# Who rounds the weight slabs while the gates are built: GpSimd alone, or ScalarE the high halves and GpSimd the low ones

## What is computed

```
experts, gates = top 16 of the key products, for 8 heads      # 128 picks for each token
a   = einsum('cd,ced->ce', h_c, u[e_c])                       # one dot product for each pick
act = gelu(a) * g_c
out = einsum('ce,ced->cd', act, v[e_c])
```

## Time and profile before

| | |
|---|---|
| time of 3 runs | 2722.94 to 2726.37 us, median 2724.3 |
| the profiled execution | 2727.47 us, its span 2725.7 us |
| granted TensorE clock, mean | 0.97 |
| PE busy | 2557.2 us (94%) |
| DVE busy | 1528.9 us (56%) |
| ACT busy | 725.1 us (27%) |
| POOL busy | 1786.2 us (66%) |
| DMA | 502.61 MB, mean 184 GB/s |

### The profile page before, as it was taken

How to read it: one execution, slowest core, us unless ns; L and a number is a source line. 1 busy time by engine, 2 the same in 40 slices (tenths; PEclk the granted TensorE clock), 3 DMA queues, 4 the chain that set the end, 5 groups by cost and what they waited for, 6 DMA issues and landing times.

```text
span 2725.7 us, 35334 instructions
## 1 busy us (share of the span) xinstructions
PE 2557.2 (94%) x12644; PEld 2132.2 (78%) x12644; DVE 1528.9 (56%) x3197; ACT 725.1 (27%) x1297; POOL 1786.2 (66%) x1315
## 2 busy tenths in 40 slices
PE   3989799999989999998889998999999989999999
PEld 2866568888757666677768898999999978888887
DVE  5447632121246325445438898877778366666665
ACT  5148511000132323433310111111212123333332
POOL 2746557666824243366556676999998668888885
PEclk8989899999989999999999998999999999999999
DMA  6224222222311011122223345899987799999995
GB/s 245 93 70 148 101 77 93 93 103 98 108 48 62 31 47 66 47 92 79 78 81 118 119 146 197 291 366 357 345 337 296 273 365 346 342 341 352 352 353 219
DMA packets 134761, 502.61 MB, mean 184 GB/s; under 512 B 11248, under 2 KB 53872, under 8 KB 103152
## 3 DMA queue, kind: packets, MB, share of 16 engines
q1 hardware_dynamic: 70832, 311.97, 31.4%
q0 software_dynamic: 36864, 134.23, 13.0%
q10 hardware_dynamic: 26944, 54.85, 5.3%
HBM read 448.58 MB, written 52.43 MB: 184 GB/s over the span
## 4 chain that ended last, share of the span: by engine, by line
PE 61%; DVE 11%; POOL 10%; DMA 9%; issue 5%; ACT 3%; ACTq 0%; SPq 0%; DVEq 0%; POOLq 0%
PE banks L566 9%; PE banks L567 9%; PE banks L568 9%; DMA raw<-weights 4%; POOL W_lo L503 3%; POOL W_lo L426 3%; PE banks L694 3%; DMA B_lo_plain<-u_rows,arena 3%; PE banks L924 2%; PE banks L926 2%; PE banks L925 2%; PE banks L839 2%; PE banks L841 2%; PE banks L840 2%; PE banks L712 2%
## 5 line engine op out<-in xcount | busy, mean ns | idle before, releaser
L451 POOL TENSOR_TENSOR W_lo<-raw,W_hi 128x512 fp32r<-128x512 f32 x376 | 493.9, 1323 | 0.0
L454 POOL TENSOR_TENSOR beat<-zero 128x1 f32<-128x1 f32 x94 | 19.8, 211 | 615.8 <-PE banks L714 215.5
L839 PE MATMUL banks<-A_hi,W_hi 128*128 128x384 f32 x1024 | 381.0, 372 | 1.2 <-issue 1.1
L841 PE MATMUL banks<-A_hi,W_lo 128*128 128x384 f32 x1024 | 346.4, 338 | 0.0
L840 PE MATMUL banks<-A_lo,W_hi 128*128 128x384 f32 x1024 | 344.5, 336 | 0.0
L426 POOL TENSOR_TENSOR W_lo<-raw,W_hi 128x2048 fp32r<-128x2048 f32 x65 | 299.4, 4606 | 5.2
L566 PE MATMUL banks<-A_hi,W_hi 128*128 128x512 f32 x680 | 267.8, 394 | 4.9 <-issue 4.9
L568 PE MATMUL banks<-A_hi,W_lo 128*128 128x512 f32 x680 | 264.7, 389 | 0.0
L567 PE MATMUL banks<-A_lo,W_hi 128*128 128x512 f32 x680 | 264.6, 389 | 0.0
L446 POOL CAST W_hi<-raw 128x512 fp32r<-128x512 f32 x376 | 247.9, 674 | 0.0
L1877 DVE TENSOR_TENSOR A_lo<-arena,A_hi 128x768 fp32r<-128x768 f32 x64 | 136.6, 2134 | 171.5 <-ACT A_hi L1362 171.4
(11 more groups left out here) (282 smaller groups left out, 6185.0 us busy)
## 6 DMA issues: line engine op xcount, KB each, us to landing
raw<-weights SPq DMA_DIRECT2D x241, 1024.0 KB, 4.9
gelu_dram<-B_plain ACTq DMA_DIRECT2D x64, 384.0 KB
gates_dram<-arena ACTq DMA_DIRECT2D x48, 512.0 KB, 10.0
arena<-gelu_dram SPq DMA_DIRECT2D x32, 768.0 KB, 8.4
arena<-gates_dram SPq DMA_DIRECT2D x32, 768.0 KB, 11.1
W_plain<-weights SPq DMA_DIRECT2D x4, 1024.0 KB, 15.9
X<-x_t SPq DMA_DIRECT2D x1, 2048.0 KB, 14.4
arena<-v_rows,arena POOLq DMA_INDIRECT x128, 7.9
```

What stands on the lines that cost most here:

```text
L451: return pool.tensor_tensor(W_lo[:, j, cols], raw[:, j, cols], W_hi[:, j, cols].bitcast(F32), ALU.subtract)
L839: mm(to, lh, rh, start=k == 0, stop=False)
L841: last = mm(to, ll, rh, start=False, stop=k == KD - 1)
```

## The change

From slab 111 on (`HIGHS_AT`), the high half of a u slab, and of the first two v slabs, is made by ScalarE with an activation (`high_of`), which signals a new semaphore `u_high`. GpSimd waits for it and makes the low half. ScalarE makes the high half of slab s+1 before the gelus of slab s. That is behind the gelus of slab s-1 and behind the two gate stores that follow them in half of the slabs; for slabs 155 and 156 it is also behind a set of four stores. Slabs up to 110 stay as they were.

```diff
+HIGHS_AT = HOT_AT + 1
...
-        slab_half, v_half = sem("slab_half"), sem("v_half")
+        slab_half, u_high, v_half = sem("slab_half"), sem("u_high"), sem("v_half")
...
             for s in range(IN_PARTS, N_MID + PAIRS + 2):
-                split_whole(s)
+                if s < HIGHS_AT:
+                    split_whole(s)
+                else:
+                    pool.wait_ge(u_high, s - HIGHS_AT + 1)
+                    low_of(s)
                 if s >= HOT_AT and n_u < SLOTS:
...
+            def high_of(s):
+
+                j = s % 2
+                act.wait_ge(slab_loaded[j], (s - j) * 8 + (8 * (N_ADA - 4) + 16))
+                act.wait_ge(slab_used, s - 1)
+                act.activation(W_hi[:, j, :], raw[:, j, :], ACT.Copy).then_inc(u_high, 1)
+
...
                 for s in range(with_tokens):
+                    high_of(N_MID + first + s + 1)
                     gelus(first + s, tokens=lambda j: tokens(2 * s + j))
                     if q:
                         per_slab = STORES // 4
...
                 for s in range(between):
                     for part in range(STORES // 2 * s, STORES // 2 * (s + 1) if s < 2 else 0):
                         store_gates(q, part)
+                    high_of(N_MID + first + with_tokens + s + 1)
                     gelus(first + with_tokens + s)
                 first += with_tokens + between
+            high_of(N_MID + PAIRS + 1)
             act.wait_ge(u_dotted, SLOTS)
             act.activation(dots, dots, ACT.Gelu).then_inc(dots_gelu, 1)
```

## The result

The changed kernel takes 2737.97 us (median of 5 runs, 2736.42 to 2742.55) against 2725.14 us for the kernel before (5 runs, 2722.94 to 2726.93): ratio 1.0052, 95% interval 1.0041 to 1.0062. By the medians it is slower by 12.8 us (11 to 17 by the interval). The forecast was 2729.7 with a range up to 2737.0. The sign held, and so did the mechanism in the gates' stage, with a loss larger than forecast. In the tail, behind the gates' stage, the forecast had nearly all of the delay absorbed, and it was not.

The account below looks back on a forecast made before the run. It took TensorE, at 10.25 us a slab, to bound the gates' stage, with 6.7 us lost to late one-hots. Profiled 2727.47 + 4.4 (stage) + 1.0 (third v slab) = 2732.9; the median lies 3.2 lower: 2729.7, range 2719 to 2737.

Parts of the forecast that it names:

- The quantity that counts is the distance from a slab's end to the first fetch: Gates' stage: late fetched rows delay dots and one-hots, so this distance sets TensorE's stalls; B + 6.8 to B + 9.2 before.
- B: The end of slab s-2, which frees the place of slab s; the prediction counts the stage's times from it.
- First fetch at B + 7.8, store slabs B + 9.1: Gates' stage after the change: GpSimd's first fetch behind cast and low half, later in slabs with gate stores.
- A fetch of 8.6 in store slabs: Gates' stage: assumed length of a first fetch in store slabs, the middle of 7.9 to 9.3 us; 6.25 in others.
- it evens out: Rival, no change: traffic sets fetch landings, stalls stay near 6.7 us, v stage absorbs the rest; 2724.3 to 2725.5; chance 0.25.
- The sum of 11.2 us in waits, with a new stall in slab 123: Gates' stage: TensorE stalls predicted in slabs 120, 130, 123, 128, 138, 144 and 145, together 11.2 us.
- Sum 11.2 us against 6.7 now: 4.4 us slower: Gates' stage: predicted stalls of 11.2 us less the 6.7 lost before, taken as a slowdown of 4.4.
- I take 1.0 us: v stage: how much later the third v slab comes, most of slab 155's 5.9 us delay absorbed; ends -3 and +6.
- its transfers start at most 1.9 later, and the fetches of v rows, which compete with them, start later too: v stage: the third v slab's transfers hardly move and face later competing fetches; the basis for 1.0 us.
- not absorbed: Rival, slower still: the tail's 5.9 us add to the stage's 4.4, giving 2734.6; chance 0.18.
- 11.9 us of waiting behind it: v stage: TensorE's waiting from 2181.39 to 2209.81, around two v slabs, held to absorb the delay.
- GpSimd was the pace: Rival, faster: relieved of 92 us, GpSimd fetches early, the stage's 6.7 us go, giving 2718.6; chance 0.12.

Follow-up runs that it names:

- high_first: Changed kernel, with each ScalarE cast directly behind the second gelu, ahead of the store's wait and issue, slabs 111 to 158: 2721.4 us.
- fetch_first: Changed kernel, with GpSimd issuing a slab's fetches ahead of its wait for ScalarE's high half: 2725.8 us.
- tail_only: Kernel before, with ScalarE making only the high halves of slabs 155 to 158: 2731.2 us, ratio 1.0023.
- only_157_158: Kernel before, with ScalarE making only the high halves of v slabs 157 and 158: 2725.4 us, ratio 1.0000.
- fetch_first_tail_undone: Changed kernel, with fetches ahead of GpSimd's wait and the high halves of slabs 155 to 158 back with GpSimd: 2719.4 us.
- tail_undone: Changed kernel, with the high halves of slabs 155 to 158 back with GpSimd: 2731.9 us, ratio 1.0024.
- sp_order: Changed kernel, with slab 160's load ahead of the reload of pairs 4 and 5 in SP's queue: 2729.9 us.
- stores_late: Changed kernel, with ScalarE's cast ahead of the set of four gate stores for slabs 155 and 156: 2733.4 us.
- before_sp_order: Kernel before, with slab 160's load ahead of the reload of pairs 4 and 5 in SP's queue: 2722.8 us.
- best: Changed kernel, with fetches ahead of GpSimd's wait, high halves of 155 to 158 on GpSimd, slab 160's load ahead of the reload: 2715.7 us.

## Why the prediction was right or wrong

- *The quantity that counts is the distance from a slab's end to the first fetch.* Right. In slabs with gate stores the mean is B + 9.4 in the changed kernel and the stage loses 17.2. It is B + 8.25 in the kernel before, with 6.7 lost, B + 7.1 in high_first with 1.5, and ahead of B in fetch_first with 0.1.
- *First fetch at B + 7.8, store slabs B + 9.1.* Nearly: 7.9, and 9.0 to 9.8 with one of 10.46. The term "issue of two gate stores (1.26)" was taken from one row; in slab 121 it is 2.55.
- *A fetch of 8.6 in store slabs.* 7.0 to 9.0, mean 8.3. The start moved and the length did not, so "it evens out" falls.
- *The sum of 11.2 us in waits, with a new stall in slab 123.* The sum is right, 11.6, and slab 123 is among them, but this is in part luck. Slab 123 was to wait 1.22 and waited 2.43, slab 145 1.28 and 1.78, while slabs 130 and 144 waited 0.5 less each than forecast. Those errors cancel.
- *"Sum 11.2 us against 6.7 now: 4.4 us slower".* This step failed; it is the smaller of the two misses. It takes a measured loss (6.7, which includes what stalls cost beyond the wait) from a sum of waits (11.2). Like against like is 11.2 - 5.4 = 5.8. The 0.25 per stall stood in my own working of slab 120 and was not used. And TensorE after a stall was priced at full clock: two falls cost 3.4 us in the profile. This part is not steady: in the four profiles with the changed stage and late fetches it lost 12.7 to 17.2 (mean 14.6, 7.9 more than before), and by the medians the stage part costs 6.6.
- *A gap of 5.9 before slab 155.* Right, 6.01; the clock fell behind it, 2.0 more.
- *"I take 1.0 us"* for the third v slab. This is the larger miss: 5.5 in the profile, 5.9 by tail_only. The step that failed is "its transfers start at most 1.9 later, and the fetches of v rows, which compete with them, start later too". The transfer that ends the wait is slab 160's load. It was issued 16.2 us later (2181.23 to 2197.45), of which 9.1 is that everything stands later by slab 153's gelu, so 7.1 later in the tail. Two things hold it. It needs the place of slab 158, whose low half ends 8.8 us later in the tail (2176.63 before, 2194.49 after). That alone puts the issue 4.2 us later, because before the load left 4.6 us behind that low half. And it is queued on SP behind a reload that waits for VectorE's products, which holds it for another 3.0. My own text had the low half of 158 end "some 8 us later", and the load that waits for it start "at most 1.9 later"; both can't be. I followed the first reload of the gates, which in the tail left 2.0 us earlier and not 1.9 later (2170.48 before, 2177.60 after), and not the load of slab 160. The fetches moved along with it, and the flight stayed about as long (21.1 and 19.6), so there was no relief from competition.
- *The rival "not absorbed", 4.4 + 5.9*, named the low half of slab 158 on the first products as what speaks for it. It is the case that came true, with the stage larger than it had. By only_157_158 that low half costs nothing by itself. Its 0.18 was too little. What I held against it, "11.9 us of waiting behind it", is only slack if what ends the wait doesn't move.
- *"GpSimd was the pace".* With this order in ScalarE's queue no. high_first (3.9 us under before) and fetch_first_tail_undone (5.9) show that most of its 6.7 were there to be had.

Not settled: why the clock fell behind waits of 1.96 and 2.43 us and not behind one of 2.58; whether the third v slab comes earlier if ScalarE takes the products' high half ahead of slab 160's cast, which was not tried; and why the stage's loss differs by 4.5 us between executions with the same stage, of which the falls of the clock are a part.

## What to carry to other kernels

Taking work from a crowded engine doesn't shorten the chain if the new engine has something in front of it in its own queue: write down, from release to dependent step, what stands ahead in every queue, because 1 to 4 us there outweighed 92 us of relief. Issue what needs no wait (here the fetches) ahead of the wait, and the cast that others wait for ahead of stores that nobody waits for yet. Before you count another engine's idle time as slack, find the transfer that ends it. Follow its issue through its in-order queue, and follow the buffer that it needs to whatever frees it.

## What the runs showed of the hardware

- A short stall of TensorE can cost more than its length. After waits of 1.96, 2.43 and 6.01 us the granted clock was at 0.50 for some microseconds, 1.7 to 2.0 us lost each time, with PE shown as busy. After the wait of 2.58 it was not. Other runs show both too: the clock fell to 0.50 behind a wait of 2.07 in tail_undone and 2.23 in sp_order, and stayed at 1.00 behind 2.44 and 2.46 in stores_late.
- The flight of one and the same 1 MB load varied fourfold. It took 19.6 us in the changed kernel, issued 2.8 us behind the first v fetch. Issued 0.12 us ahead of it, it took at most 5.0 us in sp_order, but 16.8 in before_sp_order and 17.3 in best.
- A VectorE operation with two inputs in SBUF that started 0.15 us behind a GpSimd subtraction of 128x2048 took 4.51 us instead of 0.71.
- A cast on ScalarE runs while its queue issues stores (1782.26 to 1784.18 over 1782.40 to 1784.17), so putting it ahead delays them by nothing. Behind the issues it waits for all of them, 5.78 us for six.
